# The order of the weight pairs and of VectorE's opening steps in a hybrid decoder block

## The reference

```python
u = rms_norm(x, norm_mix_pre_w)
proj = u @ w_in
z, xbc, dt_raw, q, k, v, gate_ssd, gate_attn = _split(proj, IN_SIZES)
xbc = jax.nn.silu(causal_dwconv(xbc, ssd_conv_w, ssd_conv_b))
dt = jax.nn.softplus(dt_raw + ssd_dt_bias)
q = apply_rope(q, cos, sin)
k = apply_rope(k, cos, sin)
```

## Time and profile before

| | |
|---|---|
| median of 3 runs | 2058.36 us (2055.4 to 2059.94) |
| the profiled execution | 2056.53 us |
| its span, first to last instruction | 2054.8 us |
| PE busy | 1992.1 us, 97% of the span |
| DVE busy | 1413.2 us, 69% |
| ACT busy | 988.5 us, 48% |
| POOL busy | 661.3 us, 32% |
| mean granted TensorE clock | 0.995 of full speed |

### The profile page before, as it was taken

One profiled execution on the slowest core, in us unless ns is written; L12 is line 12 of the kernel. 1 busy time (PEld: TensorE's weight loads), 2 busy tenths in 40 slices (PEclk: granted clock), 3 DMA queues, 4 the chain that ended last, 5 costly groups with the idle time before them and its releaser, 6 DMA issues. The chain is left out here.

```text
span 2054.8 us, 26989 instructions
## 1 busy us (share of the span) xinstructions
PE 1992.1 (97%) x9528; PEld 1606.6 (78%) x9528; DVE 1413.2 (69%) x1882; ACT 988.5 (48%) x1843; POOL 661.3 (32%) x473
## 2 busy tenths in 40 slices
PE   6899999999999999999899999999999999999997
PEld 6777788888767677777688888888888888888886
DVE  6777767766689888989634446579777778743523
ACT  6543344444467777777533224345344444444532
POOL 6524424423366666666300000034222222100000
PEclk9999999999999999999999999999999999999999
DMA  4244334433555445444554343221221222455443
GB/s 159 84 117 148 113 106 154 133 113 103 177 175 152 124 143 151 114 144 146 172 168 160 127 154 134 104 83 62 92 92 66 87 92 78 166 167 181 126 143 91
DMA packets 166379, 261.98 MB, mean 127 GB/s; under 512 B 18432, under 2 KB 108928, under 8 KB 166272
## 3 DMA queue, kind: packets, MB, share of 16 engines
q1 hardware_dynamic: 131728, 216.02, 32.8%
q0 software_dynamic: 8368, 30.94, 4.4%
q10 hardware_dynamic: 26176, 13.64, 2.2%
HBM read 191.73 MB, written 63.57 MB: 124 GB/s over the span
## 5 line engine op out<-in xcount | busy, mean ns | idle before, releaser
L2790 DVE TENSOR_TENSOR lt_d_lo<-lt_w_raw,lt_d_hi 128x640 fp32r<-128x640 f32 (+1 forms) x62 | 55.3, 891 | 133.8 <-ACT lt_d_hi L2489 133.6
L2360 POOL TENSOR_TENSOR lt_t_f<-lt_w_raw 128x512 f32<-128x512 f32 x21 | 29.1, 1384 | 261.9 <-DVE lt_t_lo L2718 260.3
L163 PE MATMUL ps_zg<-z_w,u_hi 128*128 128x512 f32 x256 | 109.3, 427 | 2.4 <-DVE z_w L1710 1.9
L2489 ACT ACTIVATE lt_d_hi<-lt_w_raw 128x640 fp32r<-128x640 f32 (+1 forms) x62 | 49.1, 792 | 119.1 <-PE lt_ps L165 102.2
L994 DVE TENSOR_TENSOR fr_w_lo<-fr_w_f,fr_w_hi 128x512 fp32r<-128x512 f32 x69 | 54.4, 805 | 68.5 <-ACT fr_w_hi L754 51.9
L165 PE MATMUL ps_zg<-z_w,u_lo 128*128 128x512 f32 x256 | 100.6, 393 | 0.0
L2447 ACT ACTIVATE lt_t_hi<-lt_t_f 128x512 fp32r<-128x512 f32 x84 | 52.4, 628 | 99.9 <-PE lt_ps L165 61.7
L164 PE MATMUL ps_zg<-z_w,u_hi 128*128 128x512 f32 x256 | 100.1, 391 | 0.0
L2534 ACT ACTIVATE lt_w_hi<-lt_w_raw 128x1024 fp32r<-128x1024 f32 x22 | 23.2, 1059 | 147.3 <-PE lt_ps L165 141.1
L1547 POOL TENSOR_TENSOR mx_seg<-mx_seg,mx_cbm 128x1024 f32<-128x1024 f32 x31 | 74.0, 2386 | 57.5 <-DVE mx_cbm L1743 49.9
L1523 POOL TENSOR_TENSOR mx_seg<-work,acs 128x1024 f32<-128x1024 f32 x31 | 62.1, 2002 | 88.5 <-DMA work<-feat_s 75.7
(11 more groups left out here) (552 smaller groups left out, 6809.2 us busy)
## 6 DMA issues: line engine op xcount, KB each, us to landing
lt_w_raw<-in_w_up SPq DMA_DIRECT2D x44, 512.0 KB, 4.4
work<-acs_s SPq DMA_DIRECT2D x32, 512.0 KB, 4.0
lt_sig<-gate_s SPq DMA_DIRECT2D x24, 512.0 KB, 3.6
lt_w_raw<-in_w_down SPq DMA_DIRECT2D x32, 384.0 KB, 3.2
ff_s<-lt_fo SPq DMA_DIRECT2D x21, 512.0 KB, 5.0
tok_s<-fr_xt SPq DMA_DIRECT2D x20, 512.0 KB, 3.2
lt_w_raw<-in_w_down SPq DMA_DIRECT2D x32, 320.0 KB, 3.0
work<-tok_s SPq DMA_DIRECT2D x32, 256.0 KB, 3.9
```

The costliest lines, as they stand in the source:

```text
L163: pe.matmul(dst, s_hi, m_hi, start=first, stop=False, skip_group_check=onto)
L2489: act.activation(down_w(m)[0][:, 0:n], w_raw[:, m % 2, 0:n], ACT.Copy).then_inc(dw_hi_done, 1)
L2790: dve.tensor_tensor(down_w(m)[1][:, 0:n], w_raw[:, m % 2, 0:n], down_w(m)[0][:, 0:n].bitcast(F32), ALU.subtract).then_inc(dw_lo_done, 1)
```

## The change

Two things. In `ORDER` the first two q and k pairs, ("r", 0) and ("r", 4), change places with the gate pairs ahead of them, so that each is followed by a gate pair. In the opening the clamp of the angles becomes a step of its own (`table_clamp`) ahead of the last copy of rows; the last low part of u goes ahead of the angles and of dt's opening; the low part of s2 goes behind the low parts of t3 and b11; and on ACT the sines go behind the high parts of t3 and b11.

```diff
-ORDER = (("c", 0), ("c", 1), ("g", 0), ("r", 0), ("c", 8), ("g", 1), ("r", 4), ("c", 10), ("g", 2), ("c", 2), ("c", 3),
+ORDER = (("c", 0), ("c", 1), ("r", 0), ("g", 0), ("c", 8), ("r", 4), ("g", 1), ("c", 10), ("g", 2), ("c", 2), ("c", 3),
@@ ACT, ahead of its loop
             table_u()
-            table_sin()
             hi_t3(1)
             hi_b11(1)
+            table_sin()
             hi_t1(1)
@@ DVE, the angles
-            def table_angles():
-
+            def table_clamp():
                 dve.wait_ge(ang_reduced, 1)
                 do(dve.tensor_scalar(ang[:], ang[:], 3.1415925, -3.1415925, ALU.min, ALU.max))
+
+            def table_angles():
                 do(dve.tensor_scalar(m_t[:], ang[:], -1.0, None, ALU.mult))
@@ DVE, ahead of its loop
+            table_clamp()
             rows(NT - 1)
+            split_s3(NT - 1)
             table_angles()
             table_dt_open()
-            split_s3(NT - 1)
             dve.wait_ge(s4_ready, TH)
-            low_sum(1, s2_lo, s2_f, s2_hi)
             lo_t3(1)
             lo_b11(1)
+            low_sum(1, s2_lo, s2_f, s2_hi)
             lo_t1(1)
```

## The result

The changed kernel takes 2063.68 us as a median of 12 runs (2061.18 to 2066.51). The kernel before, in runs between them, takes 2058.38 us (12 runs, 2055.4 to 2063.25). The ratio is 1.0027, with an interval of 1.0018 to 1.0035: the change makes the kernel **slower by 5.3 us**. The forecast was 2069.0 us, slower by 10.6. The sign and the cause were right, the size was twice too large.

What follows compares the result with a forecast made beforehand. PE was taken as the bound, busy but for a few long waits. Terms -5.0 - 8.2 + 23.8 = +10.6 us gave a median of 2069.0 us; own range 2064 to 2073, 8 in 10 2057 to 2074.

Steps and rivals of the forecast that it cites:

- The opening: Opening, 60 to 90 us: PE's 4.87 us wait for the last low part of u goes; gain 5.0 us.
- what is late next: Opening: once PE is early, ACT limits; its idle 2.45 + 3.27 us goes, tile 0's copy ends 5.1 us earlier.
- The q pairs: Pairs behind r0 and r4: followed by gate pairs, they no longer make PE wait for a convolution; gain 8.2 us.
- The meeting of dt and rotation: Turns 3 and 6: dt steps and POOL's sine products take turns, u3 comes late; loss 23.8 us, bounds 0 and 24.2.
- u3 at S + 23.2: Turn 3: u3 done 23.2 us after pair start S, needed at S + 13.6; PE stands 9.6 us, likewise turn 6.
- cheap quarrel: Turns 3 and 6: each of eight dt steps pays only 1.35 us; PE stands 6 us, loss 15 us in all.
- full price: Turns 3 and 6: eight dt steps wait for POOL's products, sines at 3.4 us each; PE stands 9.6 us each.
- The dt steps slip through: Rival, turns 3 and 6: POOL pays, DVE keeps its pitch, u3 at S + 13.0; -13.2, 2045.2 us; chance 0.17.
- One place harmless: Rival: one dt place costs nothing because swaps land later, or both are cheap; 2057.1 to 2060.2 us; chance 0.13.
- The opening gives nothing: Rival, opening: ACT's Exp holds the two copies behind it as long as PE did; 2074.0 us; chance 0.08.

Runs made afterwards that it cites:

- experiment 4: The kernel before with only the new order of pairs and the old opening: 2068.53 us, ratio 1.0052.
- experiment 5: The changed kernel with the old order of pairs, so only the opening differs from the kernel before: 2055.36 us, ratio 0.9986.
- experiment 1: The changed kernel with both parts of dt one turn later (turns 3 and 6 to 4 and 7), behind gate pairs: 2047.27 us, ratio 0.9948.
- experiment 2: The changed kernel with POOL's sine products cut to 8 of 1024 columns in r0 and r4, dt left in place: 2046.63 us, ratio 0.9947.
- experiment 6: The kernel before, old order and opening, with dt moved to the turns of r0's and r4's rotation (4 and 7): 2067.06 us, ratio 1.0043.
- experiment 3: The changed kernel with only the first dt steps moved from turn 3 to turn 4, the rest left in turn 6: 2057.8 us, ratio 0.9992.

## Why the prediction was right, and where its size was off

**The opening: right.** The low part starts at 64.28 and lasts 0.82 us, and PE does not wait for it. The finish of tile 0 was forecast near 81.6:

```profile
64.28 0.82 DVE L972 TENSOR_TENSOR u_lo<-fr_s_f,u_hi 128x512 fp32r<-128x512 f32 x1
...
81.50 3.92 DVE L1058 SCALAR_TENSOR_TENSOR fr_xc<-ps_zg,fr_misc,fr_xc 128x1023 f32<-128x1023 f32 x3 [0.93 <-ACT fr_xc L797]
```

Against 86.57 that is 5.07 us; forecast 5.0, bounds 4 and 5.7. ACT was what is late next, as the prediction said. In time it is worth some 4.2 us with the new order (experiment 4) and 3.7 with the old one (experiment 5). The value was a little too high: a wait of 2 us that was already in the profile can be followed by the slow clock or not.

**The q pairs: right.** Forecast 8.2 us. Experiments 1 and 5 differ by the order and the place of dt that suits it: 2055.36 against 2047.27, 8.1 us. Their traces reach pair 2 at nearly the same time (105.06 and 105.16) and pair 9 at 251.56 and 242.91, 8.75 us apart behind it. In experiment 1 the pairs behind r0 take 19.54 and 19.14 us and those behind r4 19.04 each, with no wait for a convolution.

**The meeting of dt and rotation: right in kind.** Two stops for u3, in pairs 3 and 6, each followed by a stretch at half clock, with dt steps of 1.36 to 2.50 us beside POOL's products: this is what the prediction named as its sign, and experiments 1 and 2 show the cause. The Trainium skill's rule (SBUF — State Buffer, section "Who interferes with whom"), that of two such steps the second waits until the first has ended, agrees with the rows: a dt step that starts 0.30 us behind a sine product of 2.5 us lasts 2.50 us.

**The size: the term that failed is u3 at S + 23.2.** It came at S + 20.35 in turn 3 and S + 19.75 in turn 6, so PE stood 6.64 and 6.04 us, not 9.6 each. The clock cost 2.56 us each (5.28 - 2.72), a little over the 2.3 taken and the bound of 2.5. The 6 us of the prediction's cheap quarrel come close to these waits, but by luck: there eight dt steps paid 1.35 us each; in the trace three or four paid, up to 2.50 us each, and the cosine products paid as well. Two steps of the full price were wrong.

The first is the price of a sine product. The 3.4 us came from rows of before in which DVE began a cosine product 0.04 us earlier; POOL's time held its own wait. All ten sine products of before and after, shortest, median and longest in ns, first of before, then of after:

```profile
L665 POOL TENSOR_TENSOR fr_xt<-fr_xt,fr_sin_f x10: 3372/3430/3434, 153.2 to 542.2; 128x1024 f32<-128x1024 f32 x10
```

```profile
L665 POOL TENSOR_TENSOR fr_xt<-fr_xt,fr_sin_f x10: 2483/3380/3437, 129.7 to 547.5; 128x1024 f32<-128x1024 f32 x10
```

Each row of sine products in before starts 0.04 or 0.05 us behind a cosine product, as in the earlier trace rows; that the shortest and the longest lay within 0.06 us looked like a price. The product itself takes 2.5 us. Experiment 2 shows POOL's wait at its plainest, with 8 columns per row, the first beside a dt step, the second started 0.24 us behind a cosine product:

```profile
129.45 0.32 POOL L666 TENSOR_TENSOR fr_xt<-fr_xt,fr_sin_f 128x8 f32<-128x8 f32 x1 [9.61 <-DMA fr_xt<-fr_xc]
131.57 1.04 POOL L666 TENSOR_TENSOR fr_xt<-fr_xt,fr_sin_f 128x8 f32<-128x8 f32 x1 [1.80 <-DMA fr_xt<-fr_xc]
```

The second step is where the waiting stood. The prediction let eight dt steps wait for POOL, one behind each of its six products and two behind the last, with both cosine products and the sum behind those. POOL's last product was forecast to end at 4.0 + 12.0 + 1.7 = S + 17.7; it ended at 142.32, S + 17.94, in turn 3. So POOL's end was right there by luck: its first swap landed late (S + 5.3 instead of S + 3.5), and its sines were short. But only three dt steps paid, in turn 6 four, because the others had passed before POOL began or while it stood idle for a DMA (0.57 us in turn 3; 0.39 and 0.94 us in turn 6). So the two cosine products ran in turn with POOL's subtractions (4.40 us for both, 2.37 without POOL) instead of behind them. What was left for DVE behind POOL's end was the sum and u2 and u3, 144.73 - 142.32 = 2.4 us, where the prediction had 0.7 + 3.4 + 1.4 = 5.5. The difference is 3.1 us; with POOL's end 0.24 us later than forecast it gives the 2.85 us between S + 23.2 and S + 20.35. In turn 6 POOL began at S + 3.56, as forecast, and with the shorter sines ended at 208.96, S + 16.2; 3.5 us followed.

With the measured loss in place of its 23.8, and its own two gains, the sum of the prediction would have been -5.0 - 8.2 + (6.64 + 6.04 + 2 * 2.56) = +4.6 us, against the 4.7 us between the spans. So close a match is partly luck, since the gain of the opening differs by 1.5 us and more from one execution to the next (last section).

**The rivals.** "The dt steps slip through" (2045.2 us) did not happen, but it is what experiments 1 and 2 make happen: 2047.27 and 2046.63. "One place harmless" was nearly seen in experiment 6, by the late swap that the prediction named. (Its reason for it, that at r1 the second sine waits for its swap, is not in the row: both sine products stand there in 6.77 us without idle time.) "The opening gives nothing" is out by experiments 4 and 5.

## What to carry to other kernels

Where work is put by a fixed turn number, and the list that says what stands in that turn is changed, look up what now shares the turn; here the reorder won 8 us and its meeting with an unmoved table cost 17. A duration in a profile can hold a wait for another engine: before a row is taken as a price, look at what ran beside it, and distrust a group whose rows all had the same neighbour. Where two engines take turns, reckon from the end of the longer queue and ask what the other one still has to do then: here 2.4 and 3.5 us.

## What the runs showed of the hardware

- A small step of DVE can be held for the whole of a long POOL product: 128 x 256 elements, 0.42 us alone, 2.50 us behind a sine product of 2.5 us. It goes the other way too: 128 x 8 elements on POOL, 0.32 us beside a dt step, 1.04 us behind a cosine product of 1.2 us.
- Behind waits of equal length (2.24 and 2.25 us) the granted clock was 1.00 in one execution and 0.60 in another, with the same work of PE behind them; the second costs 1.5 us. Behind the 6.6 and 6.0 us waits of the kernel after it was 0.50 for 5.28 us both times; behind experiment 3's 6.04 us wait the mean of the same 5.28 us was 0.64.
- The stretch from 30 to 45 us, where PE does the same in all kernels, had a granted clock of 1.00 in the profiled executions of before and of experiments 2, 5 and 6, and of 0.89 in those of after and of experiments 1, 3 and 4. Pair 0's first product then starts some 1.6 us later (39.04 instead of 37.44). All four slow ones have the new order, but experiment 2 has it too; whether the order has a hand in it is not shown.
- That late start does not carry through. With the new opening pair 2 starts at 103.53 and 103.35 after 0.89 (kernel after, experiment 3) and at 103.28 after 1.00 (experiment 2). With the old opening the one late execution is even ahead there: 107.19 in experiment 4, against 108.85 in before and 108.59 in experiment 6. So by pairs of traces the opening is worth anything from 2.0 us (107.19 - 105.16) to 5.6 us (108.85 - 103.28); parts of this size are not to be read off one trace.
